# Two transformer blocks on one core: the first output projection's norm in halves, and the order of splits, norms and squares around it

## The reference

```python
def first_block(x, ...):
    h = _rmsnorm(x, attn_pre_norm[l])
    dq, dk, dv, sq, sk, sv = jnp.split(h @ w_qkv[l], QKV_SPLITS, axis=-1)
    diff_o = _diff_attention(dq, dk, dv, lam, rel_bias)       # 4 heads, softmax(1) - lam * softmax(2)
    diff_o = _rmsnorm(diff_o, diff_subln[l]) * (1.0 - lam_init)
    sb_o = _rmsnorm(_stick_breaking_attention(sq, sk, sv), sb_norm[l])       # 8 heads
    mix = jnp.concatenate([diff_o, sb_o], axis=-1) @ w_o[l]
    x = x + _rmsnorm(mix, attn_post_norm[l])
    h = _rmsnorm(x, ffn_pre_norm[l])
    u = _causal_depthwise_conv(h @ w_up[l], conv_w[l], conv_b[l])
    gate, val = jnp.split(u, 2, axis=-1)                      # 2 x 2816 columns
    y = (jax.nn.gelu(gate, approximate=True) * val) @ w_down[l]
    x = x + _rmsnorm(y, ffn_post_norm[l])

def second_block(x, c, ctx, ...):
    sh1, sc1, gt1, sh2, sc2, gt2 = adaln(c, w_mod, b_mod)     # silu(c) @ w_mod + b_mod
    h = modulate(rmsnorm(x, g_pre1), sh1, sc1)
    # window attention with context keys, a Fourier mix, gates, w_out:
    x = x + gt1 * rmsnorm(merge_branches(...), g_post1)
    h = modulate(rmsnorm(x, g_pre2), sh2, sc2)
    x = x + gt2 * rmsnorm(conv_ffn(h, w_up, ...), g_post2)
```

## Time and profile before

| | before |
|---|---|
| median of 3 runs | 1442.99 us (1442.13 to 1443.58) |
| profiled execution | 1443.86 us |
| its span in the trace | 1442.1 us |
| PE busy, share of the span | 1373.7 us, 95% |
| DVE busy | 842.6 us, 58% |
| ACT busy | 630.1 us, 44% |
| POOL busy | 39.3 us, 3% |
| mean granted clock of PE | 0.979 of full speed |

### The profile page before, as it was taken

One profiled execution on the slowest core, in us unless ns is written; L12 is line 12 of the kernel. 1 busy time (PEld: TensorE's weight loads), 2 busy tenths in 40 slices (PEclk: granted clock), 3 DMA queues, 4 the chain that ended last, 5 costly groups with the idle time before them and its releaser, 6 DMA issues.

```text
span 1442.1 us, 16898 instructions
## 1 busy us (share of the span) xinstructions
PE 1373.7 (95%) x6720; PEld 1108.9 (77%) x6720; DVE 842.6 (58%) x1247; ACT 630.1 (44%) x1006; POOL 39.3 (3%) x34
## 2 busy tenths in 40 slices
PE   7999998879999999999999999999989999999995
PEld 5777765557888888888886777797878888888885
DVE  5576787458766767765846544356475553344335
ACT  5345556444445534322634544444444232333323
POOL 3000000003002200000000000000000000000000
PEclk9999999989999999999999999999999999999998
DMA  6423220232222223575031111223304432232321
GB/s 229 175 96 129 73 73 30 102 132 73 90 95 93 100 91 103 195 234 184 30 112 53 51 59 59 62 100 102 100 4 146 144 119 96 95 102 90 100 88 59
DMA packets 45611, 146.69 MB, mean 102 GB/s; under 512 B 4796, under 2 KB 11964, under 8 KB 45149
## 3 DMA queue, kind: packets, MB, share of 16 engines
q1 hardware_dynamic: 45388, 145.08, 30.0%
q10 hardware_dynamic: 144, 0.52, 0.1%
HBM read 142.18 MB, written 3.41 MB: 101 GB/s over the span
## 4 chain that ended last, share of the span: by engine, by line
PE 84%; DVE 8%; ACT 4%; DMA 2%; issue 2%; SPq 0%; DVEq 0%; ACTq 0%
PE PS L330 25%; PE PS L332 24%; PE PS L331 24%; DVE X L1614 1%; PE PS L993 1%; DVE wlo L296 1%; PE PS L984 1%; DVE mt L1608 1%; DVE G_b L1608 1%; PE PS L958 1%; PE PS L630 1%; PE PS L531 1%; PE PS L625 1%; PE PS L614 1%; DVE Hlo L1614 1%
## 5 line engine op out<-in xcount | busy, mean ns | idle before, releaser
L330 PE MATMUL PS<-Hhi,whi 128*128 128x512 f32 (+1 forms) x1104 | 433.0, 392 | 31.8 <-DVE wlo L296 11.6
L296 DVE TENSOR_TENSOR wlo<-raw,whi 128x1024 fp32r<-128x1024 f32 x206 | 252.7, 1233 | 359.5 <-ACT whi L285 359.3
L331 PE MATMUL PS<-Hlo,whi 128*128 128x512 f32 (+1 forms) x1104 | 422.7, 383 | 0.0
L332 PE MATMUL PS<-Hhi,wlo 128*128 128x512 f32 (+1 forms) x1104 | 422.3, 383 | 0.0
L285 ACT ACTIVATE whi<-raw 128x1024 fp32r<-128x1024 f32 x206 | 216.5, 1054 | 262.3 <-DMA raw<-in_w_down 116.3
L330 PEld LDWEIGHTS PS<-Hhi,whi 128*128 128x128 f32 x1104 | 211.9, 192 | 86.1 <-issue 21.9
L332 PEld LDWEIGHTS PS<-Hhi,wlo 128*128 128x128 f32 x1104 | 211.9, 192 | 40.2
L331 PEld LDWEIGHTS PS<-Hlo,whi 128*128 128x128 f32 x1104 | 212.1, 192 | 38.2 <-issue 1.0
L330 PE MATMUL PS<-Dhi,whi 128*128 128x512 f32 (+1 forms) x384 | 142.9, 372 | 0.0
L331 PE MATMUL PS<-Dlo,whi 128*128 128x512 f32 (+1 forms) x384 | 142.6, 371 | 0.0
L332 PE MATMUL PS<-Dhi,wlo 128*128 128x512 f32 (+1 forms) x384 | 142.6, 371 | 0.0
(11 more groups left out here) (382 smaller groups left out, 1818.2 us busy)
## 6 DMA issues: line engine op xcount, KB each, us to landing
raw<-in_w_up SPq DMA_DIRECT2D x88, 512.0 KB, 3.5
wm<-in_w_mod SPq DMA_DIRECT2D x48, 512.0 KB, 3.8
raw<-in_w_down SPq DMA_DIRECT2D x44, 512.0 KB, 3.5
raw<-in_w_g SPq DMA_DIRECT2D x16, 512.0 KB, 3.5
raw<-in_w_out SPq DMA_DIRECT2D x8, 512.0 KB, 3.4
raw<-in_w_o SPq DMA_DIRECT2D x8, 384.0 KB, 3.4
raw<-in_w_sq SPq DMA_DIRECT2D x4, 512.0 KB, 4.2
raw<-in_w_sk SPq DMA_DIRECT2D x4, 512.0 KB, 4.5
```

Source lines behind the costliest of these rows:

```text
L296: e.tensor_tensor(wlo[i % NS], raw[i % NS], whi[i % NS].bitcast(f32), ALU.subtract).then_inc(q["w_lo"], 1)
L330: e.matmul(o, lhs[0], rhs[0], start=first, stop=False, skip_group_check=own)
L331: e.matmul(o, lhs[0], rhs[1], start=False, stop=False, skip_group_check=own)
L332: return e.matmul(o, lhs[1], rhs[0], start=False, stop=last, skip_group_check=own)
```

## The change

1. **Attention ticks.** DVE: in tick 2 the split of the first sk1 chunk stands right after `qk_out` and ahead of the adaLN sum and the Z exponents; in tick 5 the dk1 tile is taken at the end of the tick, ahead of the adaLN adds, and not at the start of tick 6. ACT: for head ("d", 1), in tick 14, the Ln stands ahead of `sb_weights`; in ticks 15 and 16 `first_heads` (PART_O) stands ahead of `d_exps`. On both, the splits of ticks 18, 20 and 22 are gone; one chunk is split at the end of tick 15 and one in tick 20, the others in the output projection.
2. **First output projection.** Tiles o6 and o7 are made in halves, in the order 6a, 7a, 6b, 7b (O_LAST). Statistics, Ln/Exp (p0a, p0b), residual and split of the input are in halves. The first four up chunks take all of half a, then half b. The squares of the new x lie in eight tiles (sq_s) and DVE adds them after the last low part, where POOL added them as they came; their stat stands after up chunk 4.
3. **Both w_down (`down`).** For the first tile of half b, DVE copies the product to Y_A and ACT squares it from there; ACT's Ln and Exp for half a follow at once, and PE's stat for half a stands two tiles earlier.
4. **Second-block norms (`normed`).** Three buffers in place of two for the scaled tile, the low part two tiles behind; the w_out norm's stat for a four products earlier, its Ln/Exp for b one tile earlier, and the squares' sums of layer 1's half b all after the sixth tile of half a.
5. **End.** PE adds the last eight squares of half b itself, by eight matmuls with ones, where DVE added seven times and PE did one.

```diff
+    O_LAST = [(o, "") for o in range(6)] + [(6, "a"), (7, "a"), (6, "b"), (7, "b")]
+
+    def o_end(o, h):
+        return (q["wo_a"], o - 5) if h == "a" else o_done(1, o)
 
...
@@ -757,43 +770,51 @@
+        for o, h in O_LAST:
             b = o % 5
-            if o == 0:
+            if h == "b":
+                e.wait_ge(q["p_y"], o + 1)
+            elif o == 0:
...
-            out_half(o, 1, 0, b)
-            out_half(o, 1, 1, b)
...
-        e.wait_ge(q["mod"], 4)
-        post_stat(7, 7, FULL)
...
-        e.wait_ge(q["p_y"], 8)
-        for k in range(5):
+            out_half(o, 1, 0, b, h)
+            out_half(o, 1, 1, b, h)
+            if (o, h) == (6, "b"):
+                e.wait_ge(q["head_v"], 8)
+                e.wait_ge(q["mod"], 4)
+                post_stat(7, 7, HALF["a"])
+
+        e.wait_ge(q["p_y"], 10)
+        e.wait_ge(q["r_ln"], RS["p0a"])
+        post_stat(9, 7, HALF["b"])
+        for k in range(8):
             e.wait_ge(q["h_lo"], 8 + k + 1)
             for j in range(4):
-                products(e, PS[:, j, :], wtile(CH["w_up"] + j, k), hx(k), k == 0, False)
+                products(e, PS[:, j, HALF["a"]], wtile(CH["w_up"] + j, k), hxh(k, "a"), k == 0, k == 7)
+        for k in range(6):
+            e.wait_ge(q["h_lo"], 16 + k + 1)
+            for j in range(4):
+                products(e, PS[:, j, HALF["b"]], wtile(CH["w_up"] + j, k), hxh(k, "b"), k == 0, False)
+            for k in range(6, 8):
-                last = products(e, PS[:, j, :], wtile(CH["w_up"] + j, k), hx(k), False, k == 7)
+                last = products(e, PS[:, j, HALF["b"]], wtile(CH["w_up"] + j, k), hxh(k, "b"), False, k == 7)
             last.then_inc(q["w_done"], 1)
-        e.wait_ge(q["s_acc"], 7)
-        e.wait_ge(q["head_ln"], 8)
-        e.matmul(PS[:, 6, :], ones, sacc, start=True, stop=True).then_inc(q["stat"], 1)
...
@@ -804,6 +825,10 @@
+            if n == 4:
+                e.wait_ge(q["s_acc"], 7)
+                e.wait_ge(q["head_ln"], 8)
+                e.matmul(PS[:, 6, :], ones, sq_s[0], start=True, stop=True).then_inc(q["stat"], 1)
...
@@ -834,8 +859,8 @@
-                    if h == "b" and i == 3:
-                        e.wait_ge(q["p_y"], PY[post] + 9)
+                    if h == "b" and i == 1:
+                        e.wait_ge(q["p_yb"], layer + 1)
                         post_stat(PA[post] + 7, 6, HALF["a"])
...
@@ -1117,7 +1146,11 @@
-        post_stat(PA[3] + 14, 6, HALF["b"])
+        e.wait_ge(q["p_yb"], 2)
+        for i in range(8):
+            e.wait_ge(q["p_sq"], SQ[3] + 8 + i + 1)
+            last = e.matmul(PS[:, 6, HALF["b"]], ones, sq_p[i][:, HALF["b"]], start=i == 0, stop=i == 7)
+        last.then_inc(q["stat"], 1)
...
@@ -1264,24 +1298,31 @@
-            if t <= len(HALVES):
+            if t < len(HALVES):
                 split_to((LEFT[t - 1] if t else 4) + NS)
-            if t in (18, 20, 22):
-                split_to(CH["w_oa"] + (t - 16) // 2 + NS)
+            if t == 14:
+                head_log(("d", 1), dnr, 128)
             if 0 <= t - 1 < 16:
                 sb_weights(t - 1)
             if t % 4 == 1 and 5 <= t < 20:
-                head_rstd(("sb", t // 4 - 1), sbr, 64)
+                head_log(("sb", t // 4 - 1), sbr, 64)
+                head_exp(("sb", t // 4 - 1), sbr)
             if t % 4 == 2 and t >= 10:
-                head_rstd(("d", (t - 10) // 4), dnr, 128)
+                if t != 14:
+                    head_log(("d", (t - 10) // 4), dnr, 128)
+                head_exp(("d", (t - 10) // 4), dnr)
+            if t in (15, 16):
+                first_heads(O_TICK[t])
             if 0 <= d < 16:
                 d_exps(d)
             for u in ENDS.get((t, 1), []):
                 v_out(u)
-            if t in O_TICK:
+            if t in O_TICK and t > 16:
                 first_heads(O_TICK[t])
+            if t == 15 or t == 20:
+                split_to(CH["w_ob"] + 1 + (t == 20))
             if t < len(HALVES):
                 split_to(LEFT_0[t] + NS)
...
+            if (o, h) == (6, "b"):
+                post_rstd("p0a", 7, HALF["a"])
+
+        for h in "ab":
+            for c in range(8):
+                scaled(h, c)
+                if h == "a" and c == 1:
+                    post_rstd("p0b", 7, HALF["b"])
+                if h == "b" and c == 1:
+                    split_to(CH["w_up"] + 5)
+        split_to(CH["w_up"] + 6)
...
@@ -1383,6 +1432,11 @@
+                    if h == "b" and i == 0:
+                        e.wait_ge(q["p_yb"], layer + 1)
+                        act(sq_p[0][:, HALF[h]], Y_A[:, o, HALF[h]], ACT.Square, "p_sq")
+                        post_rstd(f"p{post}a", 6, HALF["a"])
+                        continue
-                    if h == "b" and i == 3:
-                        post_rstd(f"p{post}a", 6, HALF["a"])
...
@@ -1754,8 +1806,9 @@
-            for u in ENDS.get((t - 1, 1), []):
-                qk_out(u)
+            if t != 6:
+                for u in ENDS.get((t - 1, 1), []):
...
@@ -1769,14 +1822,14 @@
+            if t == 2:
+                split_to(CH["sk1"] + 1)
...
-            if t in (18, 20, 22):
-                split_to(CH["w_oa"] + (t - 16) // 2 + NS)
...
@@ -1789,6 +1842,11 @@
+            if t == 5:
+                for u in ENDS[t, 1]:
+                    qk_out(u)
+            if t == 15 or t == 20:
+                split_to(CH["w_ob"] + 1 + (t == 20))
...
         e.wait_ge(q["l_xback"], 16)
-        residual(0, "", 0, vc("g_post1", n=8))
-        residual(0, "", 1, vc("g_post1", n=8))
-        scaled_lo(0)
-        for k in range(1, 8):
-            if k < 7:
-                residual(0, "", k + 1, vc("g_post1", n=8))
-            scaled_lo(k)
+        for h in "ab":
+            for c in range(8):
+                residual(0, h, c, vc("g_post1", n=8))
+                if h == "a" and c == 0:
+                    post_sum(0, 8, 8, 6, HALF["b"])
+                    post_sum(0, 9, 9, 7, HALF["b"])
+                    scaled_lo(h, 0)
+                elif c > (h == "a"):
+                    scaled_lo(h, c - 1)
+                if h == "b" and c == 1:
+                    split_to(CH["w_up"] + 5)
+            scaled_lo(h, 7)
+        for c in range(1, 8):
+            if c > 1:
+                e.wait_ge(q["s_acc"], c - 1)
+            else:
+                e.wait_ge(q["s_sq"], 16)
+            tt(sq_s[0], sq_s[0], sq_s[c], ALU.add, "s_acc")
...
@@ -1882,6 +1959,9 @@
+            o = DN_ORDER[0]
+            e.wait_ge(q["dn_o"], 15 * layer + 9)
+            ts(Y_A[:, o, HALF["b"]], PS[:, o, HALF["b"]], 1.0, 1.0, ALU.mult, ALU.mult, "p_yb")
@@ -1893,17 +1973,17 @@
-            for c in range(9):
+            for c in range(10):
                 if c < 8:
-                    if c >= 2:
-                        e.wait_ge(q["n_lo"], n + c - 1)
+                    if c >= 3:
+                        e.wait_ge(q["n_lo"], n + c - 2)
                     elif c == 0:
                         e.wait_ge(q["x_new"], XN[layer + 1] + nth(h) + 8)
                         e.wait_ge(q["gains"], 2 if layer == 0 else 4)
-                    stt(G_abcd[c % 2][:, cols], X[:, c, cols], gains[:, c:c + 1], G_r[:, cols], ALU.mult, ALU.mult, "n_v")
-                if c:
-                    e.wait_ge(q["n_hi"], n + c)
-                    stt(Hlo[:, c - 1, cols], G_abcd[(c - 1) % 2][:, cols], shift(c - 1), Hhi[:, c - 1, cols].bitcast(f32),
+                    stt(n_v[layer][c % 3][:, cols], X[:, c, cols], gains[:, c:c + 1], G_r[:, cols], ALU.mult, ALU.mult, "n_v")
+                if c > 1:
+                    e.wait_ge(q["n_hi"], n + c - 1)
+                    stt(Hlo[:, c - 2, cols], n_v[layer][(c - 2) % 3][:, cols], shift(c - 2), Hhi[:, c - 2, cols].bitcast(f32),
                         ALU.add, ALU.subtract, "n_lo")
 
         down_sums_b(0, 1, 3)
...
@@ -2102,11 +2182,8 @@
-        down_sums_b(1, 1, 3)
         for c in range(8):
             residual(3, "a", c, P2)
-            if 2 <= c < 5:
-                down_sums_b(1, 2 * c - 1, min(2 * c + 1, 8))
         for c in range(8):
             residual(3, "b", c, P2)
```

144 lines of the change are left out of this document (78 added, 66 removed).

## The result

The changed kernel takes 1412.76 us (median of 4 runs, 1412.31 to 1413.19), the kernel before beside it 1443.28 (4 runs, 1442.13 to 1444.95): a ratio of 0.9784, 95% interval 0.9769 to 0.9799. The forecast was 1410.2, within 1403 to 1422. The profiled execution has a span of 1410.7 us, against the earlier trace rows.

The account below looks back on a forecast made before the run. PE, busy 95% of the span, was taken as the bound, so only its waits and half-clock stretches could give time; terms summed to 32.8 us, 1442.99 - 32.8 = 1410.2 us, range 1403 to 1422.

Parts of the forecast that it names:

- PART_O: Attention waits at 251.97 and 263.85: PART_O moved ahead on ACT, partly returned in a wait for DT; 1.25 us together.
- up group: Output projection, norm and up group in halves: first up product at 318.6, group ends at 343.5; gain 7.1 us.
- the wait, and half of the slow stretch behind it: PE's waits throughout: each costs its own length and half of the half-clock stretch behind it, if that goes with it.
- The price of halves: Output projection and up group: 120 full products split in two, half products at 0.1195 us; costs 1.5 us.
- I take away 2.2 of its 3.0: Half clock over 238 to 244, behind the wait for dnr's Ln: 2.2 us gained, anywhere from 0 to 3.
- I put it at the same 691.6: First w_down: half a's stat keeps its time, as DVE's sums were the limit; the place loses 0.9 us.
- Three buffers free DVE from ACT's high part: Second block's norms: with earlier statistics, 1.5 and 2.45 us off two waits plus 1.7 of slow stretch; 5.6 us.
- They cost nothing: End: PE's eight small matmuls fit before half b begins on DVE, after 6.9 us of half a; end gains 3.3.
- B: Rival: attention ticks give back half of 17.7 us through waits on DVE or ACT elsewhere; 1419 us, chance 0.17.
- D: Rival: slower than before if the half clock holds for 66 us from 318 to 384; deciding form's chance 0.03.
- C: Rival: slow stretch behind the gap at 318 goes too and w_down loses nothing; 1406.7 us, chance 0.08.
- A: Rival: the slow clock stretches, 9.0 us of the sum, stay or move; 1419.2 us, chance 0.15.

Follow-up runs that it names:

- undoing two queues: The changed kernel with DVE's earlier order in tick 2 (sk1's low part) and ticks 5 and 6 (dk1): 1420.31 us.
- DT first: The changed kernel with the split of tick 15 moved behind DT in tick 16, on ACT and DVE: 1415.13 us.

## Why the prediction was right, and where it was off

The direction, the range and the median (2.6 us off) held, and the largest terms were right in kind and size: sk1, dk1, PART_O, the late split and the up group together were forecast at 20.15 and measured 19.9. Reading "the wait, and half of the slow stretch behind it" was right for these; undoing two queues returned both. The price of halves was taken from rows and holds: PE's timeline of the changed kernel in the up group, two starts 12 half products apart,

```profile
304.22 0.28 PE L333 MATMUL PS<-Hhi,whi 128*128 128x256 f32 x1
...
305.66 0.28 PE L333 MATMUL PS<-Hhi,whi 128*128 128x256 f32 x1
```

is 1.44 us, 0.120 for one. The Trainium skill (TensorE: Matmul & The Clock Gate, Back-to-back issue gap) has a formula for the isolated gap that gives 0.109 for 256 columns; the measured 0.120 decides.

Inside the up group the forecast and the trace differ in a way that the 6.74 for 7.1 hides. The forecast said that it left the slow clock behind the gap in both kernels, but its sum for the group after, 22.9 us of products and 1.9 of waits, has no slow clock in it. The trace has 3.4 us of it from 299.4 on (window 300 to 302 above), at a cost of 1.7, and at the start of half b a wait of 0.31 only. The profile of the kernel with DT first (above) has no slow stretch there, and PE waits in it as forecast, 1.25 us at the start of half b:

```profile
318.12 0.38 PE L333 MATMUL PS<-Hhi,whi 128*128 128x256 f32 x1 [1.25 <-DVE Hlo L1668]
```

That kernel is 4.43 us behind the changed one ahead of the norm and 4.44 at the start of half b, though only one of the two ran at half clock in between. So DVE's low parts set the time of half b, and the slow clock cost nothing where PE would have waited for them.

For PART_O the forecast had subtracted the wait that the moved split would bring, and 0.8 is what was kept there. In the next tick it expected a shorter wait for dnv, 0.45; instead a wait of 1.11 us for PART_O at 261.33 went, and dnv's grew by 0.70. The three waits of before add up to 4.1, and 1.23 is what came.

At 237 the wait of 1.48 went, but a slow stretch stayed, 3.4 us long where it had been 6.8, and gave 1.3. The step "I take away 2.2 of its 3.0" was 0.9 too high.

The first w_down is where the profile is furthest from the forecast, 3.0 lost and 0.9 forecast. "I put it at the same 691.6" was said of the time of the stat, and that was right (664.73 and 26.8 us of lead are 691.5). What the step left out is what PE does meanwhile: its list had two half tiles less ahead of the stat, so it stood 2.47 us in place of 1.09, and a slow stretch of 3.4 us followed. The sums were late because ACT idled 4.26 us for a chunk of weights that nobody needed yet, and had then to catch up three tiles. Moving that split removed the wait, and that kernel is 5.8 us faster, 2.5 of them the wait. The loss on DVE's side was 0.87 (first residual at 668.11 plus 26.82, against the earlier trace rows), as forecast, and cost nothing by itself: PE came later still to its wait on Hlo at 706.45 in the earlier trace rows, which vanished. The last 1.6 us are a slow stretch at 720 that is twice as long as before's at 747.

The longer wait is a real miss of the forecast, 1.4 us, and in all nine kernels with these lists. The size of 3.0 is not: over the same stretch, 340 to 736 us of the changed kernel, the other eight lose up to 1.9 or gain up to 1.3, depending on which slow stretches they have. The median of the nine is 1.6 lost, and the changed kernel's profile is the worst of them.

The second block's norms were 4.84 for 5.6, and for another reason than given. "Three buffers free DVE from ACT's high part" is wrong: with two, nothing changes. The 2.45 at half b came from taking all eight squares' matmuls after the sixth tile, a part of the change that the sum did not name; the 1.5 ahead of half a came from the earlier statistics. The missing 0.8 is a slow stretch at 1027 that became twice as long, which costs 0.9 here because PE waits in part of it. Seven of the other profiles with the changed lists have it single, and in most of them PE gains 0.95 us more: 5.8, close to the forecast's 5.6.

The end was 2.7 for 3.3. "They cost nothing" was said of PE's eight matmuls: the first begins at 1397.15 and they take 3.6 us. PE's timeline:

```profile
1397.15 0.59 PE L1152 MATMUL PS<-G_s,ones 128*128 128x256 f32 x2
...
1399.30 1.46 PE L1152 MATMUL PS<-sq_m,ones 128*128 128x256 f32 x6
```

and DVE's at the start of half b:

```profile
1400.52 0.48 DVE L1666 SCALAR_TENSOR_TENSOR X<-G_b,small,X 128x256 f32<-128x256 f32 x1
1401.75 0.42 DVE L1660 TENSOR_TENSOR G_a<-Y_A,G_r 128x256 f32<-128x256 f32 x1 [0.74 <-ACT G_r L1164]
```

so DVE waits 0.74 for their Exp.

The 2.9 us that were ahead before the first changed instruction were in no term, and are not the change's. Some 1.3 lie before 39 us; the rest is a slow stretch at 39 to 46, less the 1.27 that the changed kernel, which has none, waits at 42.19. Kernels whose lists are the same up to there were at 60 us between 0.24 us earlier and 3.55 later than the changed kernel's profile. That profile is at the lucky end, as that of the kernel before is near the other. Windows of the kernel before:

```profile
40.00:46.00 6.00, 5.99 (x17) 4.18 (x17) 4.69 (x6) 3.48 (x6) 0.00 (x0) 0.50 0.53 220
720.00:726.00 6.00, 6.00 (x46) 5.82 (x45) 3.69 (x8) 2.64 (x6) 0.00 (x0) 1.00 0.01 3
747.00:749.00 2.00, 2.00 (x6) 1.56 (x5) 2.00 (x3) 0.08 (x1) 0.00 (x0) 0.50 0.00 0
```

At 40 to 46 the changed kernel has the full clock. The profile's agreement with the sum thus rests partly on luck at the start (2.9) that pays for bad luck in w_down and the norms; without it the trace's terms add up to 28.5; the medians, in which such luck evens out in part, differ by 30.5.

Of the rivals, B and D did not happen, nor did C: w_down lost, and the shorter slow clock behind the gap brought nothing. A happened in a small part: slow stretches stayed or became longer at 228, 720 and 1027, some 4 us together. Those behind sk1 and dk1 came back with their waits. For the one behind the half b norm that isn't shown: its wait came back without it.
